# A recurrent and sparse-attention decoder on one core: front, per-head norms and gate rows rearranged

## The chip, the cores and the metric

The kernel runs on one core of a Trainium2 chip. The metric is the device time of one execution in microseconds (us), the median of several runs. TensorE (PE, and PEld for its weight loads), VectorE (DVE), ScalarE (ACT), GpSimd (POOL) and SyncE (SP) each run a program of their own in order, and wait for each other through semaphores.

## The reference, cut to what matters

Two layers, 256 tokens of width 1024. The part touched by the change is the start of the first layer and its recurrent time mix, up to the point where the scan over time begins:

```python
sh1, sc1, ... = split(silu(c) @ ada_w[0] + ada_b[0], 6)
h = rms_norm(x, norm_g) * (1 + sc1) + sh1
xx = shift_one_token(h) - h
xr, xw, xk, xv, xa, xg = [h + xx * mu[i] for i in range(6)]
r, k, v = xr @ w_r, xk @ w_k, xv @ w_v
w_log = -softplus(-(w0 + tanh(xw @ wa) @ wb)) - 0.5
a = sigmoid(a0 + (xa @ aa) @ ab)
g = sigmoid(xg @ ga) @ gb          # ga is 1024 x 160, gb is 160 x 1024
kk = heads(k * k_k);  kk = kk / max(norm(kk, per head of 64), 1e-12)
k = k * (1 + (a - 1) * k_a)
bonus = sum(r * k * r_k, per head) * v
```

Then come the scan, the output projection, a squared-ReLU feed-forward, and the second layer with sparse attention. Nothing of those is changed.

## The kernel before

Activations are held with features on the 128 partitions: a tensor of 1024 features by 256 tokens is eight chunks (j = 0 to 7) of 128 x 256. A product with large weights is done in three fast passes: ACT rounds the weights (`weight_high`, L638, raw to whi), DVE takes the rest (`weight_low`, L1070, wlo), the same is done for the activations (`x_high` L663, `x_low` L1105), and PE multiplies hi by hi, lo by hi and hi by lo (L1670, L1672, L1673). Small products run as plain f32 matmuls, and each shows as two instructions in the trace.

SP loads the weights as 1 MB pieces into a ring of four buffers (L398): pieces 0 to 7 are the shift and scale columns of `ada_w`, pieces 8 to 19 the weights of k, r and v. A buffer is loaded again when its piece is used (`s_ada` or `s_ws`). Pieces 0 to 7 are multiplied by silu(c) on DVE, two instructions each (L1040, L1042, sums in acc and acc1), and PE adds them over the partitions (`ada_columns`, L1603). DVE then forms the scale `gm` and shift `sh` (L1050 to L1056), DVE and ACT each form four chunks of h (L1087, L656), and DVE forms xx (L1092), the mixes (L1098) and the rests.

The order in the front is this. Parameter rows and c come by 15 small loads (L384 to L387 on SP, L620 to L626 on ACT); x is the last load on ACT's queue (L627). PE turns all the rows (L1588 to L1590) when the last has landed, and only then does ACT make the sigmoid of c (L643), and DVE the factors for the pieces. ACT squares x, takes the root, and scales it (L647 to L651). After the factors, ACT rounds piece 8, and DVE forms its rest before it finishes `gm`. PE's first useful work on h is the product with the inner matrices of the decay and rate branches (L1624), then `projection(0)` to `projection(11)`, with the low-rank products, `gate_inner` (L1639), the sums of kk squared (L1700), their spread to the heads (L1706) and the gate's outer product (L1646) placed between them by hand.

Four products use little of the array. `gate_inner` has 160 outputs, done as 128 and 32, the second with a 128 x 32 weight load. Its outer product has 160 inputs, done as 128 and 32 padded with zeros to 128. The sums of kk squared give 16 outputs from eight accumulated matmuls. The spread takes 16 inputs padded to 128. Each of these is eight matmuls of 256 columns.

DVE scales k to kk (L1153) and multiplies r by the bonus weights and k (L1182); `bk_part` (L1114) and `kr` (L1119 to L1121) lay out the operands of the scan. POOL makes masks at the start, and after the last `kr` it clears the workspace of the scan (L493 to L502: state, rsx, own, parity, sv); it then sends `s_zeroed`. ACT's first copy of the scan (`copy_step`, L735) and DVE's first mask (`mask_step`, L1226) wait for `s_zeroed`, and POOL's own first step (L510) stands behind it.

## Time and profile before

| what | value |
|---|---|
| median of 3 runs | 882.16 us (877.69 to 884.79) |
| the profiled execution | 882.25 us, span 880.5 us |
| mean granted TensorE clock | 0.983 |
| PE busy in the span | 809.8 us (92%) |
| DVE busy | 663.1 us (75%) |
| ACT busy | 420.2 us (48%) |
| POOL busy | 138.4 us (16%) |
| DMA | 170.18 MB, mean 193 GB/s |

The shares are averages over stages with other limits, so the change has to be read in its own stage, the first 155 us. There the timeline shows what each engine does and what ended its idle time; the table of short windows shows the data rate and the clock.

### The profile page before, as it was taken

To read this page: it belongs to the slowest core of one execution; us is meant where nothing else is said; L and a number is where in the kernel's file an instruction comes from. 1 tells how busy PE (TensorE), PEld (TensorE's weight loads), DVE (VectorE), ACT (ScalarE), POOL (GpSimd) and SP (SyncE) were. 2 spreads that over 40 slices of the span, in tenths; PEclk is the share of its full clock that TensorE was granted. 3 is DMA by queue.
4 is the path that set the end of the run, shared out by engine and by line. 5 is a ranking of instruction groups with operands and counts; after the bars stand their busy time and mean duration, and the time that the engine had idled before them with its cause. 6 is when DMAs were issued, how large, how long until landed. Compare 5 with 4: busy or idle time off the path is not lost.

```text
span 880.5 us, 17952 instructions
## 1 busy us (share of the span) xinstructions
PE 809.8 (92%) x7613; PEld 699.9 (79%) x7613; DVE 663.1 (75%) x727; ACT 420.2 (48%) x596; POOL 138.4 (16%) x207
## 2 busy tenths in 40 slices
PE   0899999899989899999999989998889899999997
PEld 0598899787877599999998788975566799999975
DVE  4897987998977689999997674789854687555552
ACT  2269532654553734434444654238646454444441
POOL 8700014534621300000000041101110000000000
PEclk9999999999999999999999999989999999999999
DMA  8953225423250859999993586670005276655541
GB/s 312 335 167 112 85 97 172 176 99 113 99 205 1 311 211 374 378 377 376 377 366 123 192 254 202 187 256 1 1 2 190 99 283 241 192 191 191 191 144 48
DMA packets 71838, 170.18 MB, mean 193 GB/s; under 512 B 5432, under 2 KB 6736, under 8 KB 71760
## 3 DMA queue, kind: packets, MB, share of 16 engines
q1 hardware_dynamic: 68784, 160.75, 52.2%
q0 software_dynamic: 2416, 7.15, 2.7%
q8 instruction: 60, 0.98, 0.5%
q10 hardware_dynamic: 560, 1.14, 0.3%
q14 instruction: 18, 0.15, 0.1%
HBM read 166.42 MB, written 1.05 MB: 190 GB/s over the span
## 4 chain that ended last, share of the span: by engine, by line
PE 66%; DVE 22%; ACT 7%; issue 3%; DMA 2%; ACTq 0%; POOL 0%; DVEq 0%; POOLq 0%
PE ps L1724 8%; PE ps L1727 8%; PE ps L1726 8%; PE ps L1735 7%; PE ps L1737 7%; PE ps L1739 7%; DVE wlo L1070 4%; PE ps L1670 2%; PE ps L1672 2%; PE ps L1673 2%; DVE acc L1042 2%; ACT whi L638 2%; PE ps L1841 2%; DVE hfull L1354 1%; DVE tt L1241 1%
## 5 line engine op out<-in xcount | busy, mean ns | idle before, releaser
L1070 DVE TENSOR_TENSOR wlo<-raw,whi 128x2048 fp32r<-128x2048 f32 (+1 forms) x98 | 217.2, 2216 | 55.4 <-ACT whi L638 53.2
L638 ACT ACTIVATE whi<-raw 128x2048 fp32r<-128x2048 f32 (+1 forms) x98 | 179.8, 1843 | 135.1 <-DMA raw<-in_mlp_down_dram 87.5
L1724 PE MATMUL ps<-ghi,whi 128*128 128x256 f32 x576 | 164.8, 286 | 8.0 <-ACT ghi L884 4.3
L1726 PE MATMUL ps<-glo,whi 128*128 128x256 f32 x576 | 164.4, 285 | 0.0
L1727 PE MATMUL ps<-ghi,wlo 128*128 128x256 f32 x576 | 164.3, 285 | 0.0
L1724 PEld LDWEIGHTS ps<-ghi,whi 128*128 128x128 f32 x576 | 111.9, 194 | 11.3 <-issue 7.6
L1726 PEld LDWEIGHTS ps<-glo,whi 128*128 128x128 f32 x576 | 112.1, 195 | 0.5
L1727 PEld LDWEIGHTS ps<-ghi,wlo 128*128 128x128 f32 x576 | 112.0, 194 | 0.0
L1735 PE MATMUL ps<-whi,hidhi 128*128 128x512 f32 x256 | 100.8, 394 | 2.0 <-DVE wlo L1070 2.0
L1737 PE MATMUL ps<-whi,hidlo 128*128 128x512 f32 x256 | 99.8, 390 | 0.0
L1739 PE MATMUL ps<-wlo,hidhi 128*128 128x512 f32 x256 | 99.6, 389 | 0.0
L1399 DVE SCALAR_TENSOR_TENSOR acc<-late,vec,acc 128x1024 f32<-128x1024 f32 x56 | 71.9, 1285 | 2.0
L1735 PEld LDWEIGHTS ps<-whi,hidhi 128*128 128x128 f32 x256 | 48.1, 188 | 12.4 <-issue 2.9
L1739 PEld LDWEIGHTS ps<-wlo,hidhi 128*128 128x128 f32 x256 | 48.1, 188 | 10.1
L1737 PEld LDWEIGHTS ps<-whi,hidlo 128*128 128x128 f32 x256 | 48.1, 188 | 9.8 <-issue 0.5
L1670 PE MATMUL ps<-xhi,whi 128*128 128x256 f32 x192 | 55.5, 289 | 0.0
L1672 PE MATMUL ps<-xlo,whi 128*128 128x256 f32 x192 | 54.3, 283 | 0.0
L1673 PE MATMUL ps<-xhi,wlo 128*128 128x256 f32 x192 | 54.3, 283 | 0.0
L913 ACT ACTIVATE relu<-ps 128x1024 f32<-128x1024 f32 x16 | 16.4, 1027 | 73.9 <-PE ps L1727 73.9
L510 POOL TENSOR_TENSOR xc<-xtr,lm 128x256 f32<-128x256 f32 x48 | 41.1, 856 | 48.0 <-PE ps L1841 41.5
L1384 DVE TENSOR_TENSOR hid<-relu 128x1024 f32<-128x1024 f32 x16 | 19.6, 1225 | 30.3 <-ACT relu L913 30.0
L1670 PEld LDWEIGHTS ps<-xhi,whi 128*128 128x128 f32 x192 | 36.8, 192 | 1.6 <-issue 1.5
(358 smaller groups left out, 1593.4 us busy)
## 6 DMA issues: line engine op xcount, KB each, us to landing
raw<-in_mlp_up_dram SPq DMA_DIRECT2D x32, 1024.0 KB, 5.5
raw<-in_mlp_down_dram SPq DMA_DIRECT2D x32, 1024.0 KB, 5.2
raw<-in_ada_w_dram SPq DMA_DIRECT2D x24, 1024.0 KB, 6.0
late<-in_ada_w_dram SPq DMA_DIRECT2D x24, 1024.0 KB, 9.0
late<-in_kv_ada_w_dram SPq DMA_DIRECT2D x8, 1024.0 KB, 8.3
raw<-in_kv_w_dram SPq DMA_DIRECT2D x6, 1024.0 KB, 5.3
raw<-in_rw_k_dram SPq DMA_DIRECT2D x4, 1024.0 KB, 8.8
raw<-in_rw_r_dram SPq DMA_DIRECT2D x4, 1024.0 KB, 5.0
```

The lines of the kernel that those rows point to most:

```text
L638: ins = sc.activation(whi[i][:, ks, :], raw[i][:, :].rearrange("p (k n) -> p k n", k=4)[:, ks, :], ACT.Copy)
L1070: ins = dv.tensor_tensor(wlo[i][:, ks, :], raw[i][:, :].rearrange("p (k n) -> p k n", k=4)[:, ks, :], whi[i][:, ks, :].bitcast(F32), ALU.s ...
L1399: ins = dv.scalar_tensor_tensor(dst, late[a % LATE_RING][:, D * k:D * k + D], V["cs"][:, n:n + 1], dst, ALU.mult, ALU.add)
L1670: mm(out_, whi[b][:, k, cols], hi[:, k0 + k, :], start=(first and k == 0 and m % 2 == 0), stop=False, skip_group_check=True)
L1672: mm(out_, whi[b][:, k, cols], lo[:, k0 + k, :], start=False, stop=False, skip_group_check=True)
L1673: ins = mm(out_, wlo[b][:, k, cols], hi[:, k0 + k, :], start=False, stop=(last and k == 3), skip_group_check=True)
L1724: mm(out_, whi[b][:, k, cols], hi[:, k0 + k, :], start=(first and k == 0 and m % 2 == 0), stop=False, skip_group_check=True)
L1726: mm(out_, whi[b][:, k, cols], lo[:, k0 + k, :], start=False, stop=False, skip_group_check=True)
L1727: ins = mm(out_, wlo[b][:, k, cols], hi[:, k0 + k, :], start=False, stop=False, skip_group_check=True)
L1735: mm(out_, hi[:, k0 + k, rows], whi[b][:, k, cols], start=(first and k == 0), stop=False, skip_group_check=True)
L1737: mm(out_, lo[:, k0 + k, rows], whi[b][:, k, cols], start=False, stop=False, skip_group_check=True)
L1739: ins = mm(out_, hi[:, k0 + k, rows], wlo[b][:, k, cols], start=False, stop=False, skip_group_check=True)
```

## The change

c gets a load, a transpose and a semaphore of its own, and x becomes ACT's first load. The six parameter rows on SP go behind piece 0, those on ACT behind the sigmoid of c. The second half of piece 7 is multiplied on PE straight from the buffer (`slab_columns`). h, the mix of k, its rounding and its rest are made chunk by chunk, and the first projection's hi by hi and lo by hi matmuls follow each chunk (`first_high`, `first_low`). ACT makes six of the eight chunks of h, in place of four, and rounds piece 8 ahead of them. `weight_low(0)` goes behind the mixes, with its matmuls.

The 32 last gate rows are computed four times into the four quarters of the partitions, and their outer product, the spread, and the sums of kk squared use a quarter of the array's rows or columns per matmul. gb1 is loaded four times (512 KB in place of 128 KB). kk_sums moves behind projection(5), the spread behind projection(6), and the gate's outer product from behind projection(6) to behind projection(9). ACT takes over kk = k * k_k and r * r_k (eight instructions each), and DVE's last product becomes one instruction (`r_by_k`). The orders of ACT, DVE and PE in this stage are written out anew. POOL makes the scan mask earlier, and its clearing of state waits for `r_by_k` as well. The core of the diff (the wrappers that only name a step are left out):

```diff
+            sp.dma_start(crow[:, :], col(A["c"][0])).then_inc(s_crow, 16)
...
+                        if n == 7:
+                            sp.wait_ge(s_cols_ps, 2)
...
+                if p == 0:
...
-                    sp.dma_start(gb1[0:32, :], A["rw_gb"][0, P:160, :]).then_inc(s_lora_out, 16)
+                    for c in range(4):
+                        sp.dma_start(gb1[32 * c:32 * c + 32, :], A["rw_gb"][0, P:160, :]).then_inc(s_lora_out, 16)
...
+                st.do(g.memset(indq[rows, :, :].rearrange("p j c -> p (j c)")[:, e:e + 35:34], 1.0))
...
+                select(indt[32 * c:32 * c + 32, :, :].rearrange("p j (e d) -> p j e d", e=2), 0,
+                       [[-2, 2], [-1, 2], [0, N]], 1, ALU.not_equal, 1.0)

...
+            g.memset(vec[:, 112:113], 0.0).then_inc(s_const, 1)
+            cst.next()
...
             pool.wait_ge(s_kr, NCH)
+            pool.wait_ge(s_kk, RK_DONE)
             st.do(g.memset(state[:, :, :], 0.0))
...
+            st = Steps(act, c_act)
+            sc = nc.scalar
+            act.dma_start(xt[:, :, :], A["x"][0].rearrange("(b p) n -> p b n", p=P)).then_inc(s_x, 16)
+            act.wait_ge(c_dve, 1)
+            st.do(sc.activation(std, std, ACT.Sigmoid))
+            act.wait_ge(s_pt_ps, 1)
+            sc.activation(V["neg"], ps[:, 6, 0:8], ACT.Sigmoid).then_inc(s_sig_c, 1)
...
-            act.dma_start(xt[:, :, :], A["x"][0].rearrange("(b p) n -> p b n", p=P)).then_inc(s_x, 16)
...
+            act.wait_ge(s_const, IDENT_ONES)
+            act.wait_ge(c_dve, 2)
+            sc.activation(csx[:, :], ones[:, 0:N], ACT.Copy, scale=V["cs"][:, 7:8]).then_inc(s_sig_c, 1)
...
-            weight_high(0)
...
+            def h_chunk(j):
+
+                if j == 2:
+                    act.wait_ge(s_cols, 2)
+                    act.wait_ge(s_xT, 1)
+                sc.activation(hF[:, j, :], ps[:, 2 + j // 2, (j % 2) * S:(j % 2) * S + S], ACT.Identity,
+                              scale=V["gm"][:, j:j + 1], bias=V["sh"][:, j:j + 1]).then_inc(s_hA, 1)
+
+            def x_high_chunk(j):
+
+                act.wait_ge(s_mix, j + 1)
+                sc.activation(xhi[0][:, j, :], xm[0][:, j, :], ACT.Copy).then_inc(s_xhi, 1)
...
+            def kk_scaled():
+
+                act.wait_ge(s_proj_ev, 2)
+                for j in range(KC):
+                    ins = sc.activation(kkF[:, j, :], kF[:, j, :], ACT.Copy, scale=pt1[:, KKC + j:KKC + j + 1])
+                st.tell(ins, kaf)
+
+            def r_scaled():
+
+                act.wait_ge(s_l2, 3)
+                act.wait_ge(s_proj_ev, 4)
+                for j in range(KC):
+                    ins = sc.activation(prkF[:, j, :], tmpF[:, j, :], ACT.Copy, scale=pt1[:, RKC + j:RKC + j + 1])
+                ins.then_inc(s_t2, 1)
...
+            weight_high(0); h_chunk(2); h_chunk(3); x_high_chunk(0); x_high_chunk(1); h_chunk(4); h_chunk(5)
+            x_high_chunk(2); x_high_chunk(3); h_chunk(6); h_chunk(7); weight_high(1); weight_high(2)
+            x_high_chunk(4); x_high_chunk(5); x_high_chunk(6); weight_high(3); x_high_chunk(7); inner_tanh()
+            x_high(1, 0, 9); outer_sigmoid(1, sgF, W0); x_high(1, 1, 10); weight_high(4); projected(0, half(kF, 0))
+            outer_sigmoid(2, aF, A0); weight_high(5); decay_exp(); k_factor(); weight_high(6)
+            projected(1, half(kF, 1)); weight_high(7); kk_scaled(); growth_exp(); x_high(0, 0, 12); kk_squared()
+            weight_high(8); kk_deviation(); gate_sigmoid(); x_high(0, 1, 13); weight_high(9); r_half(0)
+            weight_high(10); r_half(1); v_half(0); weight_high(11); gate_copied(); r_scaled()
+
+            v_half(1)
...
                 ada_piece(4 + i, acc1, i, True)
+            loaded(v, A_AT[7])
+            st.tell(dv.scalar_tensor_tensor(acc1[:, :], raw[A_AT[7] % RING][:, 0:D], V["cs"][:, 6:7], acc1[:, :],
+                                            ALU.mult, ALU.add), T["ada"])
...
+            st.do(dv.tensor_scalar(V["omka"], pt1[:, KAC:KAC + 8], -1.0, 1.0, ALU.mult, ALU.add))
+            scale_cols(spread_column(7), pt3[:, 8:16], pt2[:, 0:8], V["gm"])
...
+            def mixed_chunks(j0, j1):
+
+                js = slice(j0, j1)
+                if j0 >= 2:
+                    v.wait_ge(s_hA, j1 - 2)
                 st.do(dv.tensor_tensor(xxF[:, js, 1:S], hF[:, js, 0:S - 1], hF[:, js, 1:S], ALU.subtract))
-                st.tell(dv.tensor_scalar(xxF[:, js, 0:1], hF[:, js, 0:1], -1.0, None, ALU.mult), T["h"])
+                first = dv.tensor_scalar(xxF[:, js, 0:1], hF[:, js, 0:1], -1.0, None, ALU.mult)
+                st.tell(first, T["h"]) if j1 == KC else st.do(first)
+                for j in range(j0, j1):
+                    m = MU["k"] + j
+                    st.tell(dv.scalar_tensor_tensor(xm[0][:, j, :], xxF[:, j, :], pt1[:, m:m + 1], hF[:, j, :], ALU.mult, ALU.add),
+                            T["mix"])
+
+            def low_chunks(j0, j1):
+
+                for j in range(j0, j1):
+                    v.wait_ge(s_xhi, j + 1)
...
+            mixed_chunks(0, 1); mixed_chunks(1, 2); mixed_chunks(2, 4); low_chunks(0, 1); low_chunks(1, 2)
+            low_chunks(2, 3); low_chunks(3, 4); mixed_chunks(4, 6); lora_mixed(); mixed_chunks(6, 8); weight_low(0)
+            mix_r(0); low_chunks(4, 5); weight_low(1); low_chunks(5, 6); low_chunks(6, 7); low_chunks(7, 8)
+            weight_low(2); mix_r(1); x_low(1, 0); decay_sum(); weight_low(3); weight_low(4); mix_g(); weight_low(5)
+            x_low(1, 1); last_decays(); mix_v(0); mix_v(1); weight_low(6); weight_low(7); k_scaled(); k_grown()
+            x_low(0, 0); kk_rnorm(); weight_low(8); kk_normed(); weight_low(9); x_low(0, 1); weight_low(10)
+            decayed([0]); kk_by_rate(); decayed(range(1, NCH)); kk_grown(); weight_low(11); ada_begun(0); r_by_k()
...
+            def slab_columns(a, b):
+
+                loaded(pe, A_AT[a])
+                for j in range(KC):
+                    ins = mm(ps[:, b, N * j:N * j + N], raw[A_AT[a] % RING][:, D + P * j:D + P * j + P], csx[:, :],
+                             start=(j == 0), stop=False, skip_group_check=True)
+                ins.then_inc(s_cols_ps, 1)
+
+            def summed_columns(src, b):
...
             def gate_inner():
                 pe.wait_ge(s_t2, 2)
-                pe.wait_ge(s_mix, 5)
-                pe.wait_ge(s_lora_out, 16 * 5)
-                for b, m0, m1 in ((4, 0, P), (5, P, 160)):
-                    for k in range(KC):
-                        ins = mm(ps[0:m1 - m0, b, 0:S], ga[:, k, m0:m1], tmpF[:, k, :], start=(k == 0), stop=(k == KC - 1))
+                pe.wait_ge(s_mix, 11)
+                pe.wait_ge(s_lora_out, 16 * 8)
+                for k in range(KC):
+                    mm(ps[:, 4, 0:S], ga[:, k, 0:P], tmpF[:, k, :], start=(k == 0), stop=(k == KC - 1))
+                for k in range(KC):
...
+            def gate_branch_outer():
+
+                for j in range(KC):
+                    mm(ps[:, 4 + j // 2, (j % 2) * S:(j % 2) * S + S], gb0[:, P * j:P * j + P], tg0[:, :],
+                       start=(j % 2 == 0), stop=False, skip_group_check=True)
+                for j in BY_QUARTERS:
+                    rows = slice(32 * (j // 2), 32 * (j // 2) + 32)
+                    ins = mm(ps[:, 4 + j // 2, (j % 2) * S:(j % 2) * S + S], gb1[rows, P * j:P * j + P], tg1[rows, :],
+                             start=False, stop=True, skip_group_check=True)
                 ins.then_inc(s_l2, 1)

...
+            def first_high(k):
+
+                if k == 0:
+                    pe.wait_ge(s_hi, 1)
+                pe.wait_ge(s_xhi, k + 1)
+                for m in range(4):
+                    mm(first_outs[m], whi[first_w][:, k, first_cols[m]], xhi[0][:, k, :], start=(k == 0 and m % 2 == 0),
+                       stop=False, skip_group_check=True)
+
+            def first_low(k):
...
+            def kk_sums():
+
+                pe.wait_ge(s_const, HEAD_TABLES)
+                pe.wait_ge(s_kks, KK_SQUARED)
+                for j in BY_QUARTERS:
+                    ins = mm(ps[16 * j - 16 * (j % 2):16 * j - 16 * (j % 2) + 32, 6, 0:S], indq[:, j % 2, :], gF[:, j, :],
+                             start=(j % 2 == 0), stop=(j % 2 == 1))
+                ins.then_inc(s_kk_ps, 1)
...
+            def kk_spread():
+
+                pe.wait_ge(s_kk, KK_RNORM)
+                pe.wait_ge(s_t1, 2)
+                for j in BY_QUARTERS:
+                    rows = slice(32 * (j // 2), 32 * (j // 2) + 32)
+                    ins = mm(ps[:, 4 + j // 2, (j % 2) * S:(j % 2) * S + S], indt[rows, j % 2, :], s16[rows, :],
+                             start=True, stop=True)
+                ins.then_inc(s_kk_ps, 1)
...
+            first_high(0); first_high(1); first_low(0); first_high(2); first_low(1); first_high(3); first_low(2)
+            first_low(3); low_rank_begun(); lora_inner(); first_weights_low(); low_rank(0); projection(1)
+            low_rank(1); projection(2); projection(3); gate_inner(); projection(4); projection(5); kk_sums()
+            projection(6); kk_spread(); projection(7); projection(8); projection(9); gate_outer(); projection(10)
             projection(11)
```

## Rows read from the trace of the kernel before

**Rows 1.** Short windows: start:end, length, busy (count) by engine, PEclk, DMA share, GB/s.
```profile
8.00:10.00 2.00, 0.00 (x0) 0.00 (x0) 0.00 (x0) 0.00 (x0) 1.80 (x4) 1.00 1.04 410
32.00:34.00 2.00, 1.42 (x5) 0.41 (x3) 1.86 (x3) 0.23 (x1) 1.80 (x4) 1.00 1.00 177
42.00:44.00 2.00, 1.60 (x4) 1.36 (x5) 1.82 (x6) 0.00 (x0) 0.00 (x0) 0.50 1.09 364
```

**Rows 2.** Timeline to 84 us: start us, us, engine, line, operation, count [idle before].
```profile
3.42 20.67 SPq L398 DMA_DIRECT2D raw<-in_ada_w_dram  x8
4.71 0.55 ACTq L627 DMA_DIRECT2D xt<-in_x_dram  x1
10.15 0.43 PE L1588 MATMUL ps<-ident,rows 120*128 120x120 f32 x1 [10.15 <-DMA rows<-in_cmp_pos_v_dram]
13.46 0.79 DVE L1040 TENSOR_SCALAR acc<-raw,vec 128x1024 f32<-128x1024 f32 x1
15.34 1.06 ACT L647 ACTIVATE junk<-xt 128x1024 f32<-128x1024 f32 x1 [2.40 <-DMA xt<-in_x_dram]
18.99 0.29 ACT L648 ACTIVATE vec<-vec 128x2 f32<-128x2 f32 x1
24.52 9.21 DVE L1042 SCALAR_TENSOR_TENSOR acc<-raw,vec,acc 128x1024 f32<-128x1024 f32 x7
...
33.77 1.91 ACT L638 ACTIVATE whi<-raw 128x2048 fp32r<-128x2048 f32 x1 [10.50 <-DMA raw<-in_rw_k_dram]
33.78 2.04 PE L1603 MATMUL ps<-ones,acc 128*128 128x112 f32 x16 [0.58 <-DVE acc L1042]
35.78 2.29 DVE L1070 TENSOR_TENSOR wlo<-raw,whi 128x2048 fp32r<-128x2048 f32 x1 [1.85 <-ACT whi L638]
38.51 2.28 DVE L1087 TENSOR_SCALAR hF<-ps,vec 128x256 f32<-128x256 f32 x4
42.40 5.15 PE L1624 MATMUL ps<-hF,waa 128*128 128x256 f32 x16 [3.13 <-DVE xxF L1093]
...
83.59 7.29 PE L1639 MATMUL ps<-tmpF,ga 128*128 128x256 f32 x32 [1.93 <-ACT aF L672]
```

**Rows 3.** The chain of work in order of time, 80 to 120 us: start, us, what.
```profile
96.83 3.56 PE ps L1700 x16
100.39 0.32 PE ps L1670
...
106.35 3.46 PE ps L1706 x16
```

**Rows 4.** Groups by line and shape, 0 to 152 us: busy, mean ns | idle before.
```profile
L1639 PEld LDWEIGHTS ps<-tmpF,ga 128*32 128x32 f32 x16 | 1.7, 110 | 1.8 <-issue 0.3
L718 ACT ACTIVATE gF<-ps 128x512 f32<-128x512 f32 x4 | 2.1, 606 | 9.3 <-PE ps L1646 9.3
```

**Rows 5.** Timeline of PE in the scan, where matmuls take parts of the array.
```profile
155.01 0.27 PE L1825 MATMUL ps<-t,idc 64*64 64x64 f32 x1 [0.75 <-POOL t L528]
...
155.49 0.22 PE L1826 MATMUL ps<-idc,t 64*64 64x64 f32 x1
...
189.00 1.15 PE L1899 MATMUL ps<-uv,bkt 128*64 128x64 f32 x32
```

**Rows 6.** Timeline at the start of the scan, PE, POOL and ACT.
```profile
142.61 0.53 POOL L493 MEMSET state<- 128x512 f32 x1 [1.80 <-DVE krF L1121]
150.92 0.95 POOL L502 MEMSET sv<- 128x1024 f32 x1
151.18 2.06 PE L1778 MATMUL ps<-krF,bk 64*128 64x128 f32 x32
152.21 1.04 ACT L735 ACTIVATE knr<-krF 64x1024 f32<-64x1024 f32 x1
153.15 1.69 ACT L802 ACTIVATE glng<-gF,pt 128x256 f32<-128x256 f32 x4
153.49 0.67 POOL L510 TENSOR_TENSOR xc<-xtr,lm 128x256 f32<-128x256 f32 x1 [1.62 <-DVE xtr L1212]
```

More of the change, by code:

```diff
@@ L466, in _, with level_mask @@
             st.do(g.memset(lm[:, :, :], 0.0))
-            for level in range(6):
+            def level_mask(level):
                 b = 1 << level
@@ L473, in _ @@
                     select(v, b - 1, [[2 * b, 32 // b], [0, b]], -1)
+            for level in range(4):
+                level_mask(level)
+            pool.wait_ge(s_cols, 2)
+            st.do(g.memset(scanmask[:, :], 1.0))
+            st.tell(g.memset(scanmask[:, :].rearrange("p (u t) -> p u t", t=N)[:, :, 0:1], 0.0), cst)
+            g.memset(vec[:, 112:113], 0.0).then_inc(s_const, 1)
+            cst.next()
+            for level in range(4, 6):
+                level_mask(level)
             st.do(g.memset(idc[:, :], 0.0))
@@ L712, in _ @@
-            sc.activation(s16[0:H, :], ps[0:H, 6, 0:S], ACT.Sqrt).then_inc(s_kks, 1)
-            weight_high(8)
-            projected(2, half(tmpF, 0))
-            weight_high(9)
-            act.wait_ge(s_l2, 3)
-            for i in range(4):
-                ins = sc.activation(gF[:, 2 * i:2 * i + 2, :].rearrange("p j t -> p (j t)"), bank(4 + i), ACT.Copy)
-            ins.then_inc(s_t2, 1)
-            weight_high(10)
-            projected(3, half(tmpF, 1))
-            weight_high(11)
@@ new lines, in gate_copied, with r_half, v_half @@
+            def gate_copied():
+                act.wait_ge(s_l2, 3)
+                for i in range(4):
+                    ins = sc.activation(gF[:, 2 * i:2 * i + 2, :].rearrange("p j t -> p (j t)"), bank(4 + i), ACT.Copy)
+                ins.then_inc(s_t2, 1)
+            def r_half(h):
+                act.wait_ge(s_l1, 2)
+                projected(2 + h, half(tmpF, h))
+            def v_half(h):
+                act.wait_ge(s_kk, KK_NORMED)
+                projected(4 + h, half(vF, h))
@@ L1147, in _ @@
-            weight_low(4)
-            v.wait_ge(s_dec, 1)
-            st.do(dv.tensor_copy(PL, sgF[:, :, :].rearrange("p j (c t) -> p c j t", t=N)[:, :, :, N - 1]))
-            weight_low(5)
-            v.wait_ge(s_proj_ev, 2)
-            for j in range(KC):
-                ins = dv.tensor_scalar(kkF[:, j, :], kF[:, j, :], pt1[:, KKC + j:KKC + j + 1], None, ALU.mult)
-                st.tell(ins, T["kk"]) if j == KC - 1 else st.do(ins)
-            v.wait_ge(s_ws, 4)
-            mix("v", xm[0], low_js)
@@ new lines, in k_grown, with kk_normed, kk_by_rate @@
+            def k_grown():
+                v.wait_ge(s_dec, 2)
+                v.wait_ge(s_l1, 2)
+                for c in range(NCH):
+                    bk_part(c, kF, True)
+            def kk_normed():
+                v.wait_ge(s_kk_ps, KK_SPREAD)
+                st.tell(dv.tensor_tensor(kkF[:, :, :].rearrange("p j t -> p (j t)"), kkF[:, :, :].rearrange(
+                    "p j t -> p (j t)"), bank(4, 4), ALU.mult), T["kk"])
+            def kk_by_rate():
+                v.wait_ge(s_t2, 2)
+                st.do(dv.tensor_tensor(aF[:, :, :], aF[:, :, :], kkF[:, :, :], ALU.mult))
@@ new lines, in kk_grown, with r_by_k, decayed, ada_begun @@
+            def kk_grown():
+                v.wait_ge(s_dec, 2)
+                for c in range(NCH):
+                    bk_part(c, aF, False)
+            def r_by_k():
+                v.wait_ge(s_t2, 4)
+                st.tell(dv.tensor_tensor(prkF[:, :, :], prkF[:, :, :], kF[:, :, :], ALU.mult), T["kk"])
+            def decayed(chunks):
+                v.wait_ge(s_proj_ev, 4)
+                v.wait_ge(s_dec, 1)
+                for c in chunks:
+                    kr(c)
+            def ada_begun(i):
+                ada_piece(8 + i, acc, i, True)
@@ L1687, in projection @@
                 weights_by_x(q, outs, xhi[i % 2], xlo[i % 2], 4 * kh, kh == 0, kh == 1)
-            projection(0)
-            lora_inner()
-            projection(1)
-            low_rank(0)
-            projection(2)
-            low_rank(1)
-            projection(3)
-            gate_inner()
-            projection(4)
-            pe.wait_ge(s_kks, KK_SQUARED)
-            for j in range(KC):
-                ins = mm(ps[0:H, 6, 0:S], ind[:, j, :], gF[:, j, :], start=(j == 0), stop=(j == KC - 1))
@@ L1701, in _ @@
-            ins.then_inc(s_kk_ps, 1)
-            projection(5)
-            pe.wait_ge(s_kk, KK_RNORM)
-            pe.wait_ge(s_t1, 2)
-            for j in range(KC):
-                ins = mm(ps[:, 4 + j // 2, (j % 2) * S:(j % 2) * S + S], indt[:, P * j:P * j + P], s16[:, :],
-                         start=True, stop=True)
-            ins.then_inc(s_kk_ps, 1)
-            projection(6)
-            pe.wait_ge(s_kk, KK_NORMED)
-            lora_outer([(gb0, tg0[:, :]), (gb1, tg1[:, :])])
-            projection(7)
```

339 lines of the change are left out of this document (161 added, 178 removed).

## The prediction

> **What bounds the kernel now.** I read the table of short windows first, then the timeline up to 84 us, then the chain of work, the groups by shape, and last the timeline where the scan starts.
>
> The front has three limits in a row. The data rate is 410 GB/s as soon as the ring is filled [rows 1], so a 1 MB piece takes some 2.6 us. DVE could not start on piece 0 before 13.46, since c comes through the common transpose at 10.15, but it then ran without a gap and ended the pieces at 33.7, when piece 8 was rounded from 33.77 on [rows 2]. A gain on DVE alone would thus have waited for data. After that the work is a chain over DVE and ACT: the rest of piece 8 (2.29 us), `gm`, h at 38.51, xx, mixes; and PE starts on h at 42.40 [rows 2]. The granted clock is 0.50 there, its lower level of 1.2 GHz, after 3.13 us in which PE idled [rows 1, 2].
>
> From 42.40 to 151.18 PE sets the end. Its only stop of note is 1.9 us before `gate_inner` [rows 2, 6]. So in this stage a us of PE work is worth a us, and what DVE and ACT do counts only where it comes late. The profiled execution took 882.25 us, 0.1 above the median of 882.16, so the sum below serves for both.
>
> **The front.** SP issues c and then piece 0 at about 1.3 instead of 3.42, and x is issued first on its queue instead of at 4.71 [rows 2]. Pieces 0 to 8 and x are 10 MB, 25.6 us at 2.56; with 0.5 MB of inner weights in the same queue 26.9. Begun 1 us after the issue, piece 8 would be there at 29.2 at the earliest; moved only by its issue, 2.1 us before 33.77, at 31.7. I take 31.3, nearer to the observed one, as the rate fell to 177 GB/s at the end of that stretch [rows 1].
>
> DVE must not be later than that. It now waits for the reciprocal behind piece 0: x at 15.34 gave a root at 18.99 + 0.29, so 4.0 us after x [rows 2]. x at half the rate beside piece 0 lands at about 8. DVE stops after piece 0 until 12.2. Then seven instructions took 9.21, 1.32 each [rows 2]: the 12.5 that are left (13, one shorter) end at 28.9. PE's sum of 2.04 us [rows 2] gives `gm` at 31.4. Piece 7's second half on PE spares DVE 1.3 us for eight matmuls that lie beside DVE's last product. The dropped rest of piece 8 takes 2.3 off this chain.
>
> ACT rounds piece 8 until 33.2 (1.91), then makes two chunks of h and one rounding, 0.42 each by the row of the same shape at 153.15 [rows 2, 6]: PE begins at 34.6 instead of 42.40, **7.8 earlier**. DVE's first two mixes are ready by then. The chunks behind them come every 0.5 to 0.9 us from DVE, and PE has 32 fast matmuls (3.8 us), the inner product and then DVE's `weight_low(0)`, which I place at 45, to wait for; PE needs it at about 46. The low clock costs as before. The small loads that are moved (14 of rows, 7 of them behind ACT's sigmoid, up to 4 us of issuing) hold back only ACT, which has x to wait for anyhow; on SP they stand behind piece 0, with three more of gb1, which push piece 11 back by perhaps 2 us, and that is needed 20 us later.
>
> **PE's work.** The sums of kk took 3.56, the spread 3.46 [rows 3]; the second half of the gate's outer product is a set of the same eight matmuls. 16 instructions of 256 columns in 3.56 are 0.222 each, or 0.056 for 64 columns. The scan has 64 x 64 matmuls on four parts of the array: 32 of them start within 0.48 us, 0.0155 each, so 3.6 at a time [rows 5]. At that rate each of the three sets costs 1.0 and 0.1 for the change of shape, 2.4 less each: **7.2**. `gate_inner` took 7.29 [rows 2]; its second half becomes 64 instructions, 4.0 at the same rate instead of 3.6, so **0.4 more**. Bounds: all at once 7.8 less and none more; one after the other nothing less and 10.6 more (64 x 0.222 against 3.6).
>
> The stop of 1.9 before `gate_inner` goes: it stood for the rate branch on ACT, which now comes before the exponentials. What is late next is the mix of g on DVE, by my count at 70 with PE there at 72. **1.9**, or nothing if DVE is 2 us later.
>
> The moves of kk and r to ACT take 3.1 and 1.8 from DVE and put 3.4 each on ACT (8 x 0.42). They lie under PE, except at the end.
>
> Sum on PE: 7.8 + 7.2 - 0.4 + 1.9 = 16.5, so the projections would end at 134.7 instead of 151.18.
>
> **The new wait.** POOL's clearing now waits for `r_by_k`, and that for `r_scaled`, and that for the gate's outer product, which now stands just two projections before the end. A projection lasts 5.96 (100.39 to 106.35 [rows 3]), so the outer product ends at 134.7 - 11.9 = 122.8. Then ACT copies the gate, 2.1 [rows 4], scales r, 3.4, DVE multiplies, 2.3 (the size of the rest of a piece), and POOL clears, from 142.61 to 150.92 + 0.95, 9.3 [rows 6]. `s_zeroed` comes at 139.9, 5.2 after PE's last projection, where it came 0.7 after it before. Behind it stand ACT's copy and all of ACT's first scan steps, DVE's masks, and POOL's own steps. ACT's copy moves from 152.21 to 139.9, 12.3 earlier, POOL's step from 153.49 to 140, 13.5 earlier [rows 6]. PE's first products of the scan are done meanwhile. I take **12.8**, and 882.25 - 12.8 = 869.5.
>
> After this, the work is the same in the same order, and the ring loads four pieces ahead as before, so I carry the gain through.
>
> **A rule weighed.** Thirty-two 128 x 64 matmuls, each with its own weight load, took 1.15 us in the scan [rows 5]. The Trainium skill, TensorE: Matmul & The Clock Gate, section "Part 3: Packing small matmuls", says that a weight load overlaps running matmuls only where its row group differs. The row doesn't agree: those loads all use every row. By the rule, `gate_inner`'s 64 loads and the 16 of the sums would run one after the other.
>
> **Rivals.**
> - *The clearing is hidden.* If the scan's start has slack elsewhere, all 16.5 count: 865.8. For it: PE can do its first products and turns meanwhile. Against it: three engines stand behind the semaphore. 0.13.
> - *x lands late.* If x shares with four pieces and lands at 13, DVE resumes at 17 and ends the pieces at 33.5 as before; PE starts at 38.8, 4.2 later than I say: 873.7. For it: x took 10.6 us before (4.71 to 15.34 [rows 2]). Against it: small rows were ahead of it then. 0.13.
> - *Weight loads of column parts don't overlap.* At 0.110 each [rows 4], 64 take 7.0 instead of 4.0, and 16 take 1.8 instead of 1.1, 3.7 more: 873.2; with pairs only elsewhere too, 875. 0.10.
> - *DVE becomes the bound.* Its list from `gm` to `r_by_k` has some 92 us of work, from 31.4 to 124 without one stop, where I place it at 128 to 130. If stops cost 3 more, 872.5. 0.12.
> - *Slower: parts of the array don't overlap at all for 32-wide shapes.* Then the three sets gain nothing and `gate_inner` loses 10.6: PE ends at 151.18 - 7.8 - 1.9 + 10.6 = 152.1, the clearing 5.2 later, 157.3 against 151.87: 887.3. It decides from the point where 64 instructions cost 5 us more than now and the sets save nothing. Against it: both scan shapes overlap [rows 5]. 0.05.
> - *The gain is given back later*, in a stage bound by data: 880. 0.05.
>
> **How the numbers follow.** 0.42 is left for my sum, 869.5, its own range 867 to 872. The range of all takes in the hidden clearing and reaches up to the pairs: 864.5 to 877, leaving out the last two rivals and tails, 0.15. About 1% (8.8 us) is what a measurement here can tell from no change. Faster by over 1% is below 873.3: the sum, the hidden clearing, most of the DVE case, half of late x and half of the column case: 0.74. Slower by over 1% is above 891, part of the serial case: 0.02. The rest is 0.24.
>
> **What would show it.** Piece 8's rounding at 31 (29 to 32) and PE's first fast matmul at 34.6; sums and spread at 1.1 each; 64 short instructions of `gate_inner` in 4; PE's last projection ending at 134.7; POOL's last clearing at 140 with ACT's first copy right behind it. It is wrong if PE stops for DVE between 40 and 130, or if DVE stands before the second piece beyond 13.

## The result and the profile after

| | median us (range, runs) | profiled execution | granted clock |
|---|---|---|---|
| before | 881.06 (877.43 to 886.73, 20) | 882.25, span 880.5 | 0.983 |
| after | 885.78 (880.57 to 891.91, 20) | 885.55, span 883.8 | 0.976 |

The ratio is 1.0054 (95% interval 1.0036 to 1.0072): 0.5% slower, within 1% of no change. I had forecast 869.5 with a range up to 877.

The front, in the timeline after (start us, us, engine, line, operation, count [idle before]; here of DVE, ACT, PE and SP's queue):

```profile
9.60 0.75 DVE L1106 TENSOR_SCALAR acc<-raw,vec 128x1024 f32<-128x1024 f32 x1 [6.33 <-DMA raw<-in_ada_w_dram]
...
13.29 7.89 DVE L1108 SCALAR_TENSOR_TENSOR acc<-raw,vec,acc 128x1024 f32<-128x1024 f32 x6 [1.42 <-DMA raw<-in_ada_w_dram]
...
30.97 1.95 PE L1728 MATMUL ps<-ones,acc 128*128 128x64 f32 x16
31.41 1.91 ACT L664 ACTIVATE whi<-raw 128x2048 fp32r<-128x2048 f32 x1 [16.91 <-DMA raw<-in_rw_k_dram]
33.02 0.17 DVE L1124 TENSOR_TENSOR vec<-ps,pt 128x8 f32<-128x8 f32 x1 [2.52 <-PE ps L1728]
36.32 0.71 PE L1827 MATMUL ps<-xhi,whi 128*128 128x256 f32 x4 [1.63 <-ACT xhi L691]
36.68 2.17 SPq L432 DMA_DIRECT2D gb<-in_rw_gb_dram  x4
38.97 0.38 SPq L401 DMA_DIRECT2D raw<-in_rw_k_dram  x1
44.66 4.06 PE L1853 MATMUL ps<-hF,waa 128*128 128x256 f32 x16
51.24 1.92 ACT L664 ACTIVATE whi<-raw 128x2048 fp32r<-128x2048 f32 x1 [5.19 <-DMA raw<-in_rw_k_dram]
54.78 0.38 ACT L715 ACTIVATE twa<-ps 64x256 f32<-64x256 f32 x1
55.69 3.69 PE L1774 MATMUL ps<-twa,wab 64*128 64x256 f32 x16 [1.62 <-ACT twa L716]
```

Piece 8 is rounded at 31.41 instead of 33.77, and PE starts on h at 36.32 instead of 42.40 [rows 2]. But piece 11 is issued only at 38.97, behind gb1's four loads, and ACT stands before its rounding until 51.24; the tanh behind it keeps PE until 55.69. Short windows of the same execution (the last figures are PEclk, DMA share, GB/s):

```profile
40.00:42.00 2.00, 2.00 (x11) 2.00 (x11) 1.86 (x5) 2.00 (x3) 0.65 (x4) 0.50 1.11 360
42.00:44.00 2.00, 2.00 (x11) 2.00 (x11) 1.90 (x4) 2.00 (x3) 0.00 (x0) 0.50 1.15 387
...
148.00:150.00 2.00, 0.80 (x29) 0.61 (x20) 1.86 (x5) 2.00 (x5) 1.40 (x3) 0.50 0.99 377
188.00:192.00 4.00, 4.00 (x111) 3.81 (x111) 1.07 (x3) 0.77 (x2) 1.34 (x2) 0.61 0.02 4
```

From 38.7 the granted clock is 0.50 (1.2 GHz) for 6.8 us; before it was so for 3.4 us from 41.9 [rows 1]. After the projections it is 0.50 again from 147.9 (6.8 us), 188.9, 219.6 and 250.3 (3.4 us each); before it fell there only at 263.8 (3.4 us).

PE's groups in the projections, 75 to 142 us (busy, mean ns | idle before):

```profile
L1768 PE MATMUL ps<-tmpF,ga 128*32 128x256 f32 x64 | 3.7, 380 | 0.0
L1765 PE MATMUL ps<-tmpF,ga 128*128 128x256 f32 x16 | 3.6, 379 | 0.0
...
L1882 PE MATMUL ps<-s,indt 32*128 32x256 f32 x16 | 1.1, 400 | 0.0
L1784 PE MATMUL ps<-tg,gb 32*128 32x256 f32 x16 | 1.1, 400 | 0.0
L1872 PE MATMUL ps<-gF,indq 128*32 128x256 f32 x16 | 1.1, 385 | 0.0
```

The parts of the array do what was forecast: 1.1 in place of the 3.56 and 3.46 of [rows 3], and 64 narrow matmuls in 3.7. The start of the scan, in the timeline of POOL and PE:

```profile
138.43 0.53 POOL L513 MEMSET state<- 128x512 f32 x1 [4.88 <-DVE prkF L1283]
...
145.05 0.95 POOL L522 MEMSET sv<- 128x1024 f32 x1
146.09 0.67 POOL L530 TENSOR_TENSOR xc<-xtr,lm 128x256 f32<-128x256 f32 x1
```
```profile
141.08 2.06 PE L1961 MATMUL ps<-krF,bk 64*128 64x128 f32 x32
143.06 1.09 PE L1974 MATMUL ps<-ident,bk 128*128 128x128 f32 x8
147.61 0.27 PE L2008 MATMUL ps<-t,idc 64*64 64x64 f32 x1 [3.46 <-POOL t L548]
```

PE has its last projection done at 141.08, 10.1 earlier than before, and POOL's first step starts at 146.09, 7.4 earlier [rows 6]. So far the change gains. Then the scan gives more than that back. PE stops in the middle of bursts of matmuls that wait for nobody (`issue`):

```profile
187.92 0.62 PE L2082 MATMUL ps<-uv,bkt 128*64 128x64 f32 x14 [2.01 <-issue]
...
218.97 0.21 PE L2043 MATMUL ps<-tt,zs 64*64 64x64 f32 x1 [3.00 <-issue]
```

and SP's queue has a mark late in the scan: its first load of rw_o, which waits until DVE has used up a ring buffer (200 to 240 us; first before, then after):

```profile
203.67 14.35 SPq L398 DMA_DIRECT2D raw<-in_ada_w_dram  x3
236.25 3.75 SPq L398 DMA_DIRECT2D raw<-in_rw_o_dram  x2
```
```profile
202.72 13.76 SPq L401 DMA_DIRECT2D raw<-in_ada_w_dram  x3
238.68 0.37 SPq L401 DMA_DIRECT2D raw<-in_rw_o_dram  x1
```

From POOL's first step to that load the scan took 82.8 us before (153.49 to 236.25) and 92.6 after: 9.8 longer with the same work. The scan isn't over at that load; PE's first product of the output projection shows its real end (first before, then after):

```profile
269.77 0.50 PE L1735 MATMUL ps<-whi,zhi 128*128 128x512 f32 x1
```
```profile
272.15 0.50 PE L1916 MATMUL ps<-whi,zhi 128*128 128x512 f32 x1
```

That is 116.3 and 126.1 us from POOL's first step, the same 9.8 longer, so the load serves as a mark for these two. The first load of mlp_up comes at 287.37 before and 289.73 after, and the end 3.3 later.

### The profile page after: what moved, and what is told of

The parts are those of the page before. It is cut to its first block, busy times and chain, and to the rows that moved or that the text cites. A ratio compares the mean times of both kernels' runs of the same rounds, so it can differ in the third digit from the quotient of the medians.

```text
span 883.8 us, 18132 instructions
## 1 busy us (share of the span) xinstructions
PE 808.4 (91%) x7674; PEld 700.3 (79%) x7674; DVE 657.6 (74%) x719; ACT 431.1 (49%) x626; POOL 130.6 (15%) x211
## 4 chain that ended last, share of the span: by engine, by line
PE 65%; DVE 19%; ACT 6%; DMA 5%; issue 3%; SPq 1%; POOL 1%; DVEq 0%; POOLq 0%; ACTq 0%
PE ps L1916 7%; PE ps L1905 7%; PE ps L1920 7%; PE ps L1918 7%; PE ps L1908 7%; PE ps L1907 7%; DVE wlo L1139 4%; PE ps L2024 2%; ACT whi L664 2%; DMA raw<-in_ada_w_dram 2%; DVE hfull L1469 1%; PE ps L1809 1%; DMA raw<-in_rw_k_dram 1%; PE ps L1812 1%; PE ps L1811 1%
## 5 line engine op out<-in xcount | busy, mean ns | idle before, releaser
L1920 PEld LDWEIGHTS ps<-wlo,hidhi 128*128 128x128 f32 x256 | 48.1, 188 | 10.2
L1809 PE MATMUL ps<-xhi,whi 128*128 128x256 f32 x176 | 50.4, 286 | 0.0
L1811 PE MATMUL ps<-xlo,whi 128*128 128x256 f32 x176 | 49.8, 283 | 0.0
L1812 PE MATMUL ps<-xhi,wlo 128*128 128x256 f32 x176 | 49.8, 283 | 0.0
L530 POOL TENSOR_TENSOR xc<-xtr,lm 128x256 f32<-128x256 f32 x48 | 39.7, 826 | 61.3 <-PE ps L2024 57.2
L1108 DVE SCALAR_TENSOR_TENSOR gt<-raw,vec,gt 128x1024 f32<-128x1024 f32 x23 | 30.9, 1344 | 8.5 <-DMA raw<-in_ada_w_dram 7.8
```

Source lines behind the costliest of these rows:

```text
L1809: mm(out_, whi[b][:, k, cols], hi[:, k0 + k, :], start=(first and k == 0 and m % 2 == 0), stop=False, skip_group_check=True)
L1811: mm(out_, whi[b][:, k, cols], lo[:, k0 + k, :], start=False, stop=False, skip_group_check=True)
L1812: ins = mm(out_, wlo[b][:, k, cols], hi[:, k0 + k, :], start=False, stop=(last and k == 3), skip_group_check=True)
L1920: ins = mm(out_, hi[:, k0 + k, rows], wlo[b][:, k, cols], start=False, stop=False, skip_group_check=True)
```

## Experiments

Each median is set against runs of the kernel before on the same chip. After itself was not run again beside them; medians of before moved from 879.5 to 881.2 between the groups of runs, so the ratios to before say more than the differences from after. "Scan" is the time from POOL's first step to the first load of rw_o, and "PE free" the time at which the projections have ended. Times within a kernel are those of one profiled execution each.

**1. Where the front's lead went.** SP loads gb0 and gb1 behind piece 11, with a semaphore of their own:

```diff
-                    sp.dma_start(gb0[:, :], A["rw_gb"][0, 0:P, :]).then_inc(s_lora_out, 16)
-                    (gb1 in four) .then_inc(s_lora_out, 16)
+                if p == 11:
+                    sp.dma_start(gb0[:, :], A["rw_gb"][0, 0:P, :]).then_inc(s_gb, 16)
+                    (gb1 in four) .then_inc(s_gb, 16)
```

> The changed kernel, with the five loads of gb0 and gb1 issued behind piece 11 instead of ahead of it, on a semaphore of their own. If the late piece 11 (landed at 51.2, with ACT's tanh queued behind its rounding) is what held PE at 55.7, then piece 11 lands by 46, the tanh ends at 50.5, PE's first low-rank outer product starts at 54.1, right behind the matmuls of the rest of piece 8, and the projections end 1.6 us earlier. Rival, PE's low clock and DVE's list hold it: nothing moves.

Measured: 879.8 us, ratio to before 0.9988 (0.9965 to 1.0012), 6 us under after. The tanh let PE go at 53.85 instead of 55.69. PE was free at 142.42 all the same, as the low clock now also held from 55.4 for 6.8 us; the profiled execution was the slowest of its ten (882.52), so where the median's 6 us lie isn't shown by it.

Then PE fills its short waits as well:

```diff
-            busy(2)
+            busy(3)
...
-            first_high(0); first_high(1); first_low(0); ...
+            first_high(0); first_high(1); busy(1, 7); first_low(0); ...
-            ... first_weights_low(); low_rank(0)
+            ... first_weights_low(); busy(2, 7); low_rank(0)
```

> As e_front_w3 (gb0 and gb1 loaded behind piece 11), and PE fills its short waits in the front with f32 matmuls of 512 columns whose result is not used: three instead of two ahead of first_high(0), one more ahead of first_low(0), and two ahead of low_rank(0), where PE waits for the tanh. Theory (the late front is one of clock): the low clock between 38 and 46 and that between 55 and 66 go or shrink by half, the projections end at 137 to 139 in place of 142.4, and the median falls by 2 to 4 us from e_front_w3, to 876 to 878. Rival (the front is bound by DVE and ACT whatever PE's clock): the projections end within 1 us of 141.5 and the median stays at 880.

Measured: 878.43 us, 0.9975 (0.9946 to 1.0005). No low clock until 144.6, and PE was free at 138.25: 4.2 earlier than in the run above and 2.8 earlier than in after. One profile could have been lucky, but the other profiles bear it out: in the four kernels of this study with the filled waits PE was free at 138.2 to 138.8, in the six that keep all waits of after's front at 140.7 to 146.3, with the low clock at other places in each. In all of them `gate_inner` to the end of the projections took 60.6 us, so the difference lies ahead of it. Unused matmuls in a wait shortened the stage, so the clock was what held it. The same six show that after's own 141.08 lies at the early end: a lead of 5 to 10 us is what that front gives. The scan was as long as above, 89.5 us, with stops of 1.51 and 2.84 and low clock at 144.6 and 212.9. The median moved by only 1.4, and the two intervals overlap; the two profiled spans differ by 3.8, as the run above was profiled in its slowest execution.

**2. The clearing.** POOL makes own16 and parity ahead of the wait for `s_kr` and `RK_DONE`:

> The changed kernel, with POOL's own and parity tables made before it waits for the last decays and for r_by_k, so that only state, rsx and sv (some 2 us) are cleared after r_by_k. Theory 1, the scan's length doesn't depend on when it starts: the clearing ends near 141 instead of 146.0, ACT's first copy follows its last copy of v at 142.3, the scan starts 3.6 us earlier and the kernel is 3.6 us faster than the changed one (about 882). Theory 2, the scan's length depends on where instruction fetches of PE meet ring loads and on the clock: the scan's start moves by the same 3.6, but the scan's length changes by anything up to 8 us either way, and the total does not follow the start.

Measured: 882.93, 1.0042 (1.0012 to 1.0072); POOL's first step at 144.92 instead of 146.09. POOL's timeline:

```profile
134.92 7.73 POOL L444 TENSOR_SCALAR_AFFINE_SELECT parity<-parity 128x128 f32<-128x128 f32 x8
142.72 0.53 POOL L519 MEMSET state<- 128x512 f32 x1
```

The eight selects of parity took 7.73 here, where DVE had a product and sums to do until 140.75, and 3.36 in after from 141.63 on. So only 1.2 of the 5.5 us of the tables were won, and PE still idled 2.65 before its first turn's products and went on at the low clock (147.0, for 6.8 us). The interval takes in the ratio of after, so no gain is shown.

**3. The scan's start.** Eight f32 matmuls of 512 columns, unused, behind the first turns:

```diff
-            prep_step(0, 0); prep_step(0, 1); turn_step(0, 0); turn_step(0, 1); start_step(0, 0)
+            prep_step(0, 0); prep_step(0, 1); turn_step(0, 0); turn_step(0, 1); kept(); start_step(0, 0)
```

> The changed kernel, with eight f32 matmuls of 512 columns (3.4 us) put on PE at the start of the scan, where it idles from 144.2 to 147.6; their results are overwritten. If the low clock from 148 to 155 lengthens the scan, its first chunk gets 2 to 3 us shorter and the total 2 to 3 us less. If the scan's first chunk is bound by POOL and DVE, the clock stays at 2.4 GHz and the total is the same or, from the added work, up to 1 us more. The 32 added instructions also shift PE's instruction fetches; if those decide, the total moves without regard to the clock.

Measured: 885.79, 1.0053 (1.0019 to 1.0086). The clock stayed at 1.00 through the whole scan, and the scan took 86.2 instead of 92.6. The total is no better, since this time the low clock behind the wait for tanh held from 56.8 for 10.2 us and PE was free only at 146.25.

The 6.4 us in the scan can't be put down to the clock at its start. POOL's sixteenth instruction of line L530 stands 25.6 us behind its first here and 26.9 in after, so 1.3 are won there; the other 5.1 come later, where the stop at 187.92 is missing (the 32 added instructions also move PE's fetches, see below) and no low clock follows the stop that is left. Even the 1.3 is doubtful: after has two stops of 0.69 and 0.65 in that stretch. The run with the shifted fetches of experiment 4 has none there and low clock from 152.6 for 6.8 us. First it, then this run, over the same 598 matmuls (this one has nine of the unused ones besides):

```profile
150.60:176.00 25.40, 20.67 (x598) 17.51 (x598) 21.94 (x35) 16.14 (x32) 13.36 (x20) 0.87 0.37 132
```
```profile
151.00:176.50 25.50, 23.33 (x607) 17.72 (x607) 21.97 (x35) 15.91 (x32) 12.94 (x19) 1.00 0.35 124
```

The granted clock was 0.87 against 1.00, and the work took 25.4 and 25.5. So at the scan's start these unused matmuls won nothing that shows.

**4. PE's stops in mid-burst.** They have a mark in common. Counted through PE's instructions in the trace (weight loads, matmuls and waits), they come at 3777, 5313 and 6849 in after and at 4545, 6593 and 7617 in before: each is 193 more than a multiple of 256. The trace also has reads of 16 KB on a queue named instruction, 61 of them in after for 15,669 instructions of PE, so one for every 256. One falls on each stop; here the DMA view from 185.6 to 188 us of after:

```profile
DMA packets 3, 0.02 MB, mean 9 GB/s; under 512 B 1, under 2 KB 1, under 8 KB 2
...
q8 instruction: 1, 0.02, 2.5%
q1 hardware_dynamic: 2, 0.00, 1.2%
```

It begins at 185.72 and takes 0.97 us; the last packet of a 1 MB piece had begun at 185.57. PE stops from 185.92 to 187.92, 2.20 after that begin. The same holds for all such stops of 0.75 us or more in every kernel of this study up to 300 us: PE goes on 2.2 to 2.8 us after the read has begun. Where it began earlier than that, there is no stop. Theory A: the read stands behind the data of a ring load, and PE runs dry. First every ring load in two halves of 512 KB, issued one behind the other:

> The changed kernel, with every 1 MB ring load issued as two of 512 KB. PE's stops of 2.0 us at 185.9 and 3.0 at 216.0 lie in the middle of a burst and end 1.3 to 1.5 us after a fetch of its instructions that starts only when a 1 MB load has ended. Theory A, a fetch waits for the load that is under way: with half the load the stops get 1 to 2 us shorter, and the scan 2 to 6 us. Theory B, the fetch waits until no load is left in the queue: the stops stay as they are. SP issues 0.4 us more per piece, which should cost nothing.

Measured: 886.71, 1.0062 (1.0032 to 1.0092), stops of 1.82, 2.72 and 1.38, at most 0.4 shorter where 1 to 2 were expected; the scan took 90.3. Halves that follow each other at once are hardly less in the way. Then almost no data during the scan:

```diff
+                part = kind == "A" and a >= 8 and a < 20
-                sp.dma_start(dst, src)
+                sp.dma_start(dst[:, 0:1, 0:128] if part else dst, src[:, 0:1, 0:128] if part else src)
```

> The kernel after, but the twelve pieces of ada_w that are used during the scan are loaded as 64 KB (their first 128 columns) instead of 1 MB, and DVE reads those columns eight times over for each row of 1024; so DVE does the same number of elements and the shift and scale columns of later stages are not the reference's. Theory A (PE stops in mid-burst because an instruction fetch waits behind a 1 MB load): the stops of 2.0, 3.0 and 1.8 us near 186, 216 and 247 go, the low clock behind them too, and the first load of rw_o is issued 6 to 9 us earlier than 238.7, at 230 to 233. Theory B (the stops come from where PE's own instructions lie and loads play no part): the stops stay over 1.5 us each, and rw_o is issued at 237 or later.

Measured: 879.52, 0.9971 (0.9942 to 1.0000), 6.3 under after. The stops at 3777 and 5313 are gone, and with them all low clock between 156 and 579. SP's queue from 200 to 240 us:

```profile
200.68 14.01 SPq L403 DMA_DIRECT2D raw<-in_ada_w_dram  x3
232.90 7.41 SPq L403 DMA_DIRECT2D raw<-in_rw_o_dram  x3
```

The scan took 84.1. The stop at 6849 stays (1.76 us at 241.3), where the 1 MB loads of rw_o run. The same edit on the kernel before:

> The kernel before with the same edit of the twelve loads in the scan (64 KB each, DVE reads them eight times over; the later shift and scale columns are wrong). Theory A: before had only three stops of 1 us in the scan, so rw_o is issued 2 to 4 us earlier than 236.25, and the scan is then as long as in the kernel after with the same edit, within 2 us once the low clock at its start is taken out. Theory B: rw_o stays at 236 within 1 us, and the scan of before stays 7 us or more shorter than that of after with the same edit.

Measured: 881.06, 1.0010 (0.9981 to 1.0039), scan 81.9 against 82.8. Before had hardly anything to lose there. That leaves 2.2 us between the two. Only the scan of after still has a low clock, at 149.4 for 6.8 us, but the combined kernel with small loads (experiment 5), which has no low clock before 244.9, took 83.5; so the clock explains 0.6 of it at most, as far as two profiles can tell; the rest stays open. Then the borders themselves are moved, by sixteen matmuls of 8 columns (64 instructions) in the front of after:

> The kernel after with sixteen matmuls of 8 columns (64 of PE's instructions) put in where PE waits in the front, so that the borders at which its instructions are fetched fall 64 instructions earlier in its work. The stops of 2.0 and 3.0 us came at instructions 3777 and 5313 of the engine. Theory A (a stop needs a fetch that meets a load): the stops move by 64 instructions and their lengths change, since the fetches meet the loads at other times; the median may change by up to 4 us either way. Rival (the stops belong to that place of the scan, whatever is fetched): they stay at the same matmuls, near 186 and 216 us, as long as they were.

Measured: 885.18, 1.0044 (1.0018 to 1.0070). The long stop is again at instruction 5313, so 64 earlier in the work, in another product (PE's timeline):

```profile
218.68 0.27 PE L2097 MATMUL ps<-qb,uv 128*64 128x64 f32 x1 [3.19 <-issue]
```

The one at 3777 is gone, and a stop of 0.83 is at 4289. The stop belongs to the fetch, not to the place. Theory A stands for the scan as far as this: loads must be near for a long stop. Taking all profiles with ring loads at full size, whole or in halves, there are 198 such borders between the scan's start and 236 us. 94 had at least 0.5 MB of ring data in the 4 us ahead of the last read, and 18 of these were stops of 0.75 us or more, all those of over 1.1 us among them; of the 104 others 2 were (0.98 in before, 0.83 here). With the small loads none of 57 was. So a load ahead is not enough for a stop: 76 of the 94 borders passed without one. Nor is it always needed: behind 236 us, stops at 255 and 267.5 us, 1.31 (e_front_clock) and 1.95 (this one), and that of before at 260.6 (again in e_before_paced, at 260.5) had none ahead. What held those fetches back stays open, as does how a load holds back a fetch.

**5. All together.** gb0 and gb1 behind piece 11, the filled waits, the early tables, and six matmuls at the start of the scan:

> All of it together: gb0 and gb1 behind piece 11, the filled waits in the front, the clearing's tables made before its wait, and six f32 matmuls of 512 columns at the start of the scan. If the three parts are what the change lacked and they add up: from the kernel after 6 us for the first (885.8 to 879.8), 3 for the clearing, 3 for the front's clock, 3 to 6 for the clock at the start of the scan, so 868 to 872. If later low clock or later stops give it back, as happened to the gain of the change: 876 to 880.

Measured: **876.08 us** (871.71 to 877.94), 0.9933 (0.9908 to 0.9959): 5.1 under the 881.17 of before in the same runs and 9.7 under after, the fastest of all with whole loads. That is the range named for the case that later low clock or stops give part of the gain back. Its timeline (PE, POOL, SP's queue) and two windows:

```profile
51.50 1.88 PE L1737 MATMUL ps<-xt,ident 128*128 128x512 f32 x4
53.31 3.72 PE L1776 MATMUL ps<-twa,wab 64*128 64x256 f32 x16
...
138.73 2.06 PE L1964 MATMUL ps<-krF,bk 64*128 64x128 f32 x32
```
```profile
142.97 0.67 POOL L532 TENSOR_TENSOR xc<-xtr,lm 128x256 f32<-128x256 f32 x1
```
```profile
227.31 12.58 SPq L402 DMA_DIRECT2D raw<-in_rw_o_dram  x4
```
```profile
40.00:42.00 2.00, 2.00 (x19) 2.00 (x18) 1.84 (x5) 2.00 (x3) 0.91 (x5) 1.00 1.12 362
144.00:148.00 4.00, 4.00 (x60) 2.06 (x60) 3.76 (x8) 2.88 (x7) 3.19 (x5) 1.00 0.97 365
```

PE does 19 matmuls in the two microseconds where after did 11. The lead over before is 12.5 us at PE's last projection, 10.5 at POOL's first step, 8.9 at rw_o, 6.8 at mlp_up (280.60), and 5.7 in the span. Its one stop before 236 us is 0.80 long, at 3777; why it is so short and the one at 5313 missing was not tested, and nothing in the kernel was made to avoid them. With the small loads on top:

> As e_combined with the twelve loads of the scan cut to 64 KB, as in e_loads_small (the later shift and scale columns are wrong). It bounds what loads cost the scan when the clock is kept at its start. Theory A: e_combined had only one stop of 0.8 us at such a fetch before 240, so little is left: rw_o issued at 225.5 to 227.5, total 1 to 2 us under e_combined. Rival (loads slow the scan in other ways too, by DVE's or ACT's access to memory): 3 us or more under it.

Measured: 874.46 (4 runs), 0.9933 (0.9913 to 0.9952), the same ratio as with whole loads; scan 83.5 against 84.3. Once the long stops are missed, loads cost the scan less than 1 us. Last, the combined kernel and the kernel before with the scan's loads paced, each half issued only when the one ahead has landed:

```diff
+                    if kind == "A" and 8 <= a < 20:
+                        sp.wait_ge(...)      # the half or the piece ahead has landed
```

> As e_combined, and each of the twelve ring loads used during the scan is issued as two of 512 KB, the second only when the first has landed, and the first only when the load before it has, so that an instruction fetch never has more than 512 KB in front of it. Theory A (fetches queue behind the data of loads): no stop of PE in the middle of a burst is over 1.5 us before 240, the scan is up to 2 us shorter than e_combined's (rw_o issued at 225 to 227.5), and the median is 1 to 3 us lower, 873 to 875. Rival (the stops of e_combined are none of that kind, or the slower loads are then late for DVE): 876 or more.

> The kernel before with the same pacing of the twelve loads. Theory A: its stops in the scan were 1 us each and no low clock followed them, so at most 2 us are won: 879 to 881. Rival (pacing is worth the same to every order): 3 us or more, as in the kernel after with small loads.

Measured: 878.6, 0.9994 (0.9969 to 1.0018), and 886.77, 1.0061 (1.0037 to 1.0085). Pacing made both kernels about 0.6% slower. The combined one still had stops of 1.13 and 1.59, each with 0.52 MB in the 4 us ahead of its fetch, against the expectation of none over 1.5. So 512 KB at a time doesn't prevent them. The two profiled executions (876.32 and 881.03) are among the fastest of their kernels and show no loss, so what the pacing costs in the others stays open.

## Why the prediction was wrong

The forecast put PE free at 134.7 and carried the lead of the scan's start, 12.8, to the end. Measured: 141.08, a lead of 7.4, and an end 3.3 later in the span.

- *Piece 8 at 31.3, x early.* Right: 31.41, and ACT has x by 7.17.
- *"DVE stops after piece 0 until 12.2".* It stood until 13.29, and for the load of piece 1, not for x; that is beyond the 13 that the prediction named as a sign of being wrong. So the pieces ended at 30.10 instead of 28.9.
- *"PE's sum of 2.04 us gives `gm` at 31.4".* Too early by 1.6. Of that 1.2 are DVE's, as just said; the rest is PE's own order: the sum started at 30.97, behind the slab's sixteen instructions (29.24) and, ahead of those, five unused products from 24.79. So PE began at 36.32, not 34.6: 6.1 earlier than before instead of 7.8.
- *"The low clock costs as before".* This failed. PE arrived in pieces, with stops of 1.63, 0.37 and 1.24, and the low clock held 6.8 us instead of 3.4, 1.7 more by the estimate that half the time is lost at half the clock.
- *"push piece 11 back by perhaps 2 us, and that is needed 20 us later".* This failed too. It was needed by ACT before the tanh, and ACT runs in order: 5.19 of idle there, 1.62 of PE. With all that the lead at `gate_inner` was 1.2 (81.66, where PE arrived before, against 80.51) instead of 7.8, and the parts close: 1.7 from the late start, 1.6 from the two stops of 0.37 and 1.24, 1.7 from the clock and 1.62 from the tanh. The runs of experiment 1 bear out the last two: gb out of the way let PE go 1.8 earlier, and filled waits took the low clock out.
- *PE's work, 7.2 less and 0.4 more.* Right: from the start of `gate_inner` to the end of the projections PE took 67.6 before and 60.6 after, 7.0 less against 6.8. The Trainium skill, TensorE: Matmul & The Clock Gate, section "Part 3: Packing small matmuls", would have 64 loads that share their rows follow one another; at the 110 ns of one load that is 7.0 us against 3.7 measured, so the trace disagrees here too.
- *The stop before `gate_inner`, 1.9.* Right. 1.2 + 1.9 + 7.0 is the 10.1 measured.
- *The new wait, `s_zeroed` 5.2 after PE.* 4.9 measured, in part by luck: the clearing started 2.7 before PE was free, not 4.1, and took 7.6, not 9.3. What I missed is what that wait does to PE: it idled from 144.16 to 147.61, where it idled 0.75 before, and went into the scan at half its clock. By experiment 3 that clock cost the scan little.
- *"After this, the work is the same in the same order ... so I carry the gain through."* This step failed worst and cost the most, 9.8 us. The work was the same, but not how it fell on PE's instruction fetches and on the clock. Up to the rw_o mark after has stops of 2.01 and 3.00, and of 0.69 and 0.65, against one of 0.98 before, and low clock of 3.4 us behind each of the long ones. Small loads took the two long stops and the low clock behind them away, and 8.5 us off the scan; the same loads took 0.9 off the scan of before. All parts together, with small loads, came to 9.1 less, within 1 us of before at the mark. At the scan's real end it is 118.6 us against 116.3, so something of it stays open.

None of the rivals was this one. The nearest, "given back later", had 0.05 and looked for it in a stage bound by data; it lay in one where PE stops in mid-burst, by way of the fetches and the clock. Its chance should have been higher: the lead put PE in front of engines that were not ahead with it, so it had to become waits, and what the clock does behind a wait stood in [rows 1] already. The stops couldn't be forecast from the rows; before's own were under 1 us. One sum of the rivals is off as well: 157.3 against 151.87 is 5.4 more, so 887.7 and not 887.3.

## What to carry to other kernels

A gain made ahead of a long stage counts only as far as that stage stays as long as it was, so measure the stage itself, from its first step to its real end, before and after. When it grows with the same work, look first for stops of PE that wait for nobody, and whether a packet of the instruction queue stands beside each. Where PE arrives ahead of other engines and gets its work in pieces, fill the short waits with unused matmuls, and check in the trace that it won time: it did in the front, and not at the start of the scan. When a load is added to a queue, ask which engine, running in order, stands before the next load's data, not when that data's last user needs it. And don't credit a stage's whole difference to the one thing that was changed in it: added instructions also move the fetches.

## What the runs showed of the hardware

PE's stops in mid-burst, 0.8 to 3.2 us long, come only at fixed borders of its instruction stream (193 past a multiple of 256, in all kernels of this study), and end 2.2 to 2.8 us after a 16 KB read has begun; in before the three were 0.96 to 0.98 us, in after up to 3.00. The two long ones before the rw_o mark went with the loads. A stop is not always followed by low clock: of the fifteen of 1.9 us or more up to 300 us, in all profiles, nine had it begin between 0.8 us before their end and 1.5 behind it, and six had none, as this one of e_scan_clock, where the clock stayed at 1.00:

```profile
218.93 0.21 PE L2043 MATMUL ps<-tt,zs 64*64 64x64 f32 x1 [2.68 <-issue]
```

The Trainium skill, Runtime: NRT & Kernel Launch, section "Instruction fetch mechanics", tells of blocks of 256 instructions fetched through a queue of their own, which fits the borders, and holds that the fetch is mostly hidden; here it is hidden at most borders, and not where it begins late.

The low clock also lies at other places from one profile to the next, where the front's work is the same: behind the wait for tanh it held for 0 us in after and 10.2 in e_scan_clock, and PE was free at 141.08 and 146.25. Whether the build decides that or each execution isn't shown, as each kernel has one profile; the executions of after alone range from 880.57 to 891.91. So the medians, and not one profile, decide between versions 2 us apart.
